# Decoder step: tokens turned once in the loading stage, with the inverse norm spread by a product with ones

## The chip, the cores and the metric

The kernel runs on one core of a Trainium2 chip. The metric is the device time of one execution in microseconds (us), the median of several. For this kernel a difference under 0.2% (about 3.9 us) can't be told from no change.

## The reference, cut to what matters

The program is one layer of a decoder for 256 prompt tokens and 64 sample tokens together (T = 320), width D = 2048. Only its first two steps bear on the change:

```python
def rmsnorm(x, g):
    xf = x.astype(F32)
    y = xf * lax.rsqrt(jnp.mean(xf * xf, axis=-1, keepdims=True) + NORM_EPS)
    return (y * g.astype(F32)).astype(x.dtype)
...
    h = rmsnorm(x, lp['ln_mix_g'])
    proj = h @ lp['w_in']
```

What follows is an RWKV-7 recurrence, latent attention, an output projection, cross-attention to 256 memory tokens, and a mixture of experts (32 experts, each with three weight matrices of 2048 x 512).

## The kernel before

The kernel is written engine by engine: each stage is a block in which the queues of TensorE (PE), VectorE (DVE), ScalarE (ACT), GpSimd (POOL) and SyncE (SP) are listed by hand and wait for each other by counting semaphores. A block ends for all engines together, so the next stage starts when the last engine of this one has finished. There is no planner: the order in the text is the order on the engine.

**The loading stage** is `load_front`. The tokens lie in three tiles (`TILE`: 128, 128 and 64 tokens, with all 2048 features in a row: `x`, in the trace `x_tokens`). The stage makes, with features on the partitions: `xT`, the raw tokens turned (in the trace `rw_vak`), which are parked in DRAM for the residual; `hT` (`mix`), normalised and multiplied by the norm's weights; and `hT` as a high part `S.xh` (`x_high`) in a reduced format and a remainder `S.xl` (`x_low`). Both halves feed the projection, which makes three products for each tile of weights: high by high, high by low, low by high.

- SP issues the identity, the three tiles of tokens, the first two tiles of the projection's weights (L318), and the rest of the tables (L172).
- PE turns each raw tile, 16 transposes into four banks `p_r` (`turn_raw`, L189), the old shift state (28 small transposes, L209) and the vector rows, among them the norm's weights (L213). Then it turns each tile a second time after scaling (`turn_scaled`, L202), into three banks `p_s`.
- ACT issues the small loads, squares and sums each tile and takes the root (`square`, L239 and L241), copies the raw turned tiles out of PSUM (`copies`, L247), and rounds `hT` to its high part (`high`, L253).
- DVE takes the reciprocal of the root (L270), scales the tile's rows by it (`scale`, L273), multiplies the turned scaled tile by the norm's weights while it takes it out of PSUM (`gain`, L279), subtracts for the low part (`low`, L285), and last copies the shift state (L302).

**The projection stage** is `project_in`, the block behind it: 35 tiles of weights (s = 0 to 34), two buffers. For each, ACT rounds the high part (`split`, L457), DVE subtracts the low part (`split`, L528), and PE makes three times 16 products of 320 columns (L426, L428, L431). SP first issues two small weights and the parking of `xT` (L362 to L364), then each next tile of weights as soon as DVE has made the low part of the tile that lies in its buffer:

```python
                sp.dma_start(S.xT_dram, S.xT[:, :, :].rearrange("p t n -> p (t n)")).then_inc(parked, 16)
                for s in range(RAWS, total):
                    sp.wait_ge(low, s - RAWS + 1)
                    load_in_weights(sp, d, S, s)
```

Of the kernel before, what the change touches and what calls it, by code (L numbers as in the profile page):

```python
# [12 lines left out]
ALU = mybir.AluOpType  # L13
# [129 lines left out]
def load_front(nc, d, S):  # L143

    with ExitStack() as ctx:
# [4 lines left out]
        ss = sb("x_ss", [128, 3]); root = sb("x_root", [128, 3]); inv = sb("x_inv", [128, 3])  # L150
        p_r = [ps(f"p_r{i}") for i in range(4)]; p_s = [ps(f"p_s{i}") for i in range(3)]; p_v = ps("p_v")
        cleared = sem("cleared"); rows_in = sem("vec_in"); x_in = [sem(f"x_in{i}") for i in range(3)]; prev_in = sem("prev_in"); tables_in = sem("tables_in"); ident_in = sem("ident_in")
        vec_turned = sem("vec_turned"); vec_done = sem("vec_done"); prev_turned = sem("prev_turned"); prev_done = sem("prev_done")
        raw_turned = sem("raw_turned"); raw_copied = sem("raw_copied"); squared = sem("x_squared"); rooted = sem("x_rooted"); inverted = sem("x_inverted"); scaled = sem("x_scaled")
        turned = sem("x_turned"); gained = sem("x_gained"); high_made = sem("x_high_made"); low_made = sem("x_low_made")
# [6 lines left out]
        with nc.Block() as block:  # L162
# [12 lines left out]
            @block.gpsimd  # L175
            def _(pool):
                pool.memset(rows[:, :, :], 0.0).then_inc(cleared, 1)
                pool.memset(S.eps[:, :], EPS).then_inc(cleared, 1)

            @block.tensor  # L180
            def _(pe):
                def turn_raw(i):
                    n = TILE[i]
                    pe.wait_ge(x_in[i], 16)
                    for q in range(4):
                        if i:
                            pe.wait_ge(raw_copied, 4 * (i - 1) + q + 1)
                        for t in range(4):
                            ins = pe.transpose(p_r[q][:, n * t:n * t + n], x[0:n, i, 512 * q + 128 * t:512 * q + 128 * t + 128], S.ident[0:n, 0:n])  # L189
                        ins.then_inc(raw_turned, 1)  # L190

                def turn_scaled(i):
                    n = TILE[i]
                    pe.wait_ge(scaled, i + 1)
                    for q in range(4):
                        use = 4 * i + q
                        if use >= 3:
                            pe.wait_ge(gained, use - 2)
                        elif use == 2:
                            pe.wait_ge(vec_done, 1)  # L200
                        for t in range(4):
                            ins = pe.transpose(p_s[use % 3][:, n * t:n * t + n], x[0:n, i, 512 * q + 128 * t:512 * q + 128 * t + 128], S.ident[0:n, 0:n])  # L202
                        ins.then_inc(turned, 1)

                pe.wait_ge(ident_in, 16)
                turn_raw(0)
                pe.wait_ge(prev_in, 16)
                for t, (c, n) in enumerate(cols):
                    ins = pe.transpose(p_v[0:n, 8 * t:8 * t + 8], prev[:, c:c + n], S.ident[0:8, 0:8])  # L209
                ins.then_inc(prev_turned, 1)  # L210
                pe.wait_ge(rows_in, 16 * (len(VECTORS) + 2))
                for i in range(2):
                    ins = pe.transpose(p_s[2][:, 128 * i:128 * i + 128], rows[:, i, :], S.ident)  # L213
                ins.then_inc(vec_turned, 1)
                turn_raw(1)
                turn_scaled(0)
                turn_raw(2)
                turn_scaled(1)
                turn_scaled(2)

            @block.scalar
            def _(act):
                act.dma_start(prev[:, :], d['state_rwkv_shift'][0]).then_inc(prev_in, 16)
# [19 lines left out]
                def copies(i):  # L243
                    n = TILE[i]
                    for q in range(4):
                        act.wait_ge(raw_turned, 4 * i + q + 1)
                        act.copy(xT[:, 4 * q:4 * q + 4, at[i]:at[i] + n], p_r[q][:, 0:4 * n].rearrange("p (t n) -> p t n", t=4)).then_inc(raw_copied, 1)  # L247

                def high(i):
                    n = TILE[i]  # L250
                    act.wait_ge(gained, 4 * i + 4)
                    act.wait_ge(squared, 3)
                    act.copy(S.xh[:, :, at[i]:at[i] + n], hT[:, :, at[i]:at[i] + n]).then_inc(high_made, 1)  # L253

                square(0)
                copies(0)
                square(1)
                square(2)
# [3098 lines left out]
```

## Time and profile before

| | |
|---|---|
| median of 3 runs | 1936.49 us (1932.57 to 1936.51) |
| the profiled execution, its own time | 1926.11 us |
| its span (first to last instruction) | 1924.4 us |
| PE busy | 1795.4 us, 93% of the span |
| DVE busy / ACT busy | 687.8 us (36%) / 481.6 us (25%) |
| loading stage | to 33.84 us of the span |
| projection, first product | 35.65 us |

Times inside the trace are counted from the start of the span. In a timeline row the first number is the start, the second the time from it to the end of the last instruction merged into the row; "xN" is how many there are, and brackets hold how long the engine was idle before and what released it. Where several rows of one engine overlap, the next instruction has started while the one before is still finishing. L numbers are lines of the kernel.

### The profile page before, as it was taken

What the parts mean: (1) busy time and instruction counts of PE and PEld (TensorE: products, weight loads), DVE (VectorE), ACT (ScalarE), POOL (GpSimd) and SP (SyncE); (2) the same over time, 40 slices, a digit from 0 to 9 for tenths busy, and PEclk for the clock granted to TensorE, in tenths of its full rate; (3) what the DMA queues carried; (4) which work ended last, traced back from release to release, by engine and by line L of the source; (5) the groups of instructions that cost most, each with busy time, mean ns of one, the idle gap of its engine ahead of it and who ended that gap; (6) DMA issues with size and microseconds to landing.
All of it is one profiled execution on the core that took longest, in us unless ns stands there. A gap on an engine that the chain in (4) does not pass through costs nothing. (4 is left out here: it accounts for less than half of the span.)

```text
span 1924.4 us, 35948 instructions
## 1 busy us (share of the span) xinstructions
PE 1795.4 (93%) x15607; PEld 1232.4 (64%) x15607; DVE 687.8 (36%) x1296; ACT 481.6 (25%) x836; POOL 111.7 (6%) x115
## 2 busy tenths in 40 slices
PE   5999998997989999998999999999999999999995
PEld 5999987875667799786455554554554544555442
DVE  4437776545568443753411111111111111111113
ACT  4446654441223322732311011011110000000001
POOL 0000002300101000000000000000000000000000
PEclk8999999998999999999999999999999999999998
DMA  7644550224535772547899999999999999999997
GB/s 225 162 127 127 136 132 11 69 36 126 167 117 221 235 191 67 184 136 303 309 385 428 421 424 427 424 421 418 422 421 427 421 425 420 419 426 423 422 426 267
DMA packets 191391, 545.99 MB, mean 284 GB/s; under 512 B 39227, under 2 KB 146844, under 8 KB 163566
## 3 DMA queue, kind: packets, MB, share of 16 engines
q1 hardware_dynamic: 184080, 518.03, 70.4%
q0 software_dynamic: 6768, 26.09, 4.4%
q8 instruction: 84, 1.38, 0.3%
q10 hardware_dynamic: 438, 0.32, 0.1%
q14 instruction: 21, 0.17, 0.0%
HBM read 524.86 MB, written 28.06 MB: 287 GB/s over the span
## 5 line engine op out<-in xcount | busy, mean ns | idle before, releaser
L2976 PE MATMUL p_u<-w_expert,xgT 128*64 128x256 f32 x2048 | 239.2, 387 | 26.7 <-DMA w_expert<-in_w_up_dram 26.6
L2976 PE MATMUL p_g<-w_expert,xgT 128*64 128x256 f32 x2048 | 232.1, 379 | 1.7 <-DVE xgT L3079 0.9
L2976 PEld LDWEIGHTS p_u<-w_expert,xgT 128*64 128x64 f32 x2048 | 148.9, 140 | 108.7 <-DMA w_expert<-in_w_up_dram 33.7
L2992 PE MATMUL p_y<-w_expert,hidT 128*64 128x512 f32 x960 | 217.5, 595 | 0.5 <-DVE hidT L3091 0.5
L2976 PEld LDWEIGHTS p_g<-w_expert,xgT 128*64 128x64 f32 x2048 | 146.7, 137 | 89.1 <-issue 18.4
L2944 PE MATMUL p_xg<-low,slot_sel 128*64 128x512 f32 x768 | 177.1, 596 | 0.0
L2992 PEld LDWEIGHTS p_y<-w_expert,hidT 128*64 128x64 f32 x960 | 66.3, 137 | 125.4 <-issue 124.7
L3084 DVE CAST row<-rowf 128x1 int32<-128x1 f32 x32 | 4.9, 154 | 356.9 <-POOLq L3225 356.9
L3171 ACT ACTIVATE act_g<-p_g 128x256 f32<-128x256 f32 x32 | 12.3, 383 | 442.0 <-PE p_u L2976 442.0
L2944 PEld LDWEIGHTS p_xg<-low,slot_sel 128*64 128x64 f32 x768 | 52.3, 137 | 79.4 <-issue 73.6
L426 PE MATMUL in_acc<-x_high,w_in_high 128*128 128x320 f32 (+2 forms) x560 | 93.2, 319 | 8.2 <-ACT w_in_high L457 8.2
L3222 POOL DMA_INDIRECT x_dram<-y_slots,row x31 | 48.3, 1557 | 870.7 <-DVE y_slots L3095 870.7
L528 DVE TENSOR_TENSOR w_in_low<-w_in_raw,w_in_high 128x2048 fp32r<-128x2048 f32 (+2 forms) x35 | 77.8, 2228 | 52.4 <-ACT w_in_high L457 52.3
L3079 DVE COPY xgT<-p_xgT 128x512 f32<-128x512 f32 x32 | 22.1, 692 | 206.4 <-PE p_xgT L2959 206.4
L426 PEld LDWEIGHTS in_acc<-x_high,w_in_high 128*128 128x128 f32 (+2 forms) x560 | 84.9, 187 | 11.4 <-ACT w_in_high L457 8.9
L431 PE MATMUL in_acc<-x_high,w_in_low 128*128 128x320 f32 (+2 forms) x560 | 88.0, 309 | 1.6 <-DVE w_in_low L528 1.6
L428 PE MATMUL in_acc<-x_low,w_in_high 128*128 128x320 f32 (+2 forms) x560 | 87.8, 309 | 0.0
L431 PEld LDWEIGHTS in_acc<-x_high,w_in_low 128*128 128x128 f32 (+2 forms) x560 | 83.2, 185 | 2.3 <-DVE w_in_low L528 2.1
L428 PEld LDWEIGHTS in_acc<-x_low,w_in_high 128*128 128x128 f32 (+2 forms) x560 | 83.3, 185 | 0.2
L457 ACT CAST w_in_high<-w_in_raw 128x2048 fp32r<-128x2048 f32 (+2 forms) x35 | 64.7, 1852 | 10.6 <-DMA w_in_raw<-in_w_in_dram 4.6
L3164 ACT COPY xg<-p_xg 128x512 f32<-128x512 f32 x32 | 18.7, 585 | 190.7 <-PE p_xg L2944 190.7
L3095 DVE COPY y_slots<-p_y 128x512 f32<-128x512 f32 x32 | 22.1, 692 | 97.2 <-PE p_y L2992 97.2
(601 smaller groups left out, 2439.1 us busy)
## 6 DMA issues: line engine op xcount, KB each, us to landing
w_expert<-in_w_gate_dram SPq DMA_DIRECT2D x64, 2048.0 KB, 21.6
w_expert<-in_w_up_dram SPq DMA_DIRECT2D x64, 2048.0 KB, 23.2
w_expert<-in_w_down_dram SPq DMA_DIRECT2D x60, 2048.0 KB, 19.8
w_in_raw<-in_w_in_dram SPq DMA_DIRECT2D x32, 1024.0 KB, 5.8
ho_raw<-in_w_out_dram SPq DMA_DIRECT2D x12, 1024.0 KB, 6.5
q_lat<-in_w_out_dram SPq DMA_DIRECT2D x4, 1024.0 KB, 8.1
mem_k_s<-in_cache_mem_k_dram SPq DMA_DIRECT2D x8, 512.0 KB, 7.5
mem_v_s<-in_cache_mem_v_dram SPq DMA_DIRECT2D x8, 512.0 KB, 11.5
```

The lines of the kernel that those rows point to most:

```text
L426: pe.matmul(o, wh[s % 2][:, k, 0:m], S.xh[:, k, :], start=(k == 0), stop=False)
L428: pe.matmul(o, wh[s % 2][:, k, 0:m], S.xl[:, k, :], start=False, stop=False)
L431: ins = pe.matmul(o, wl[s % 2][:, k, 0:m], S.xh[:, k, :], start=False, stop=(k == DT - 1))
L457: act.copy(wh[s % 2][:, :, 0:m], S.raw[s % RAWS][:, :, 0:m]).then_inc(high, 1)
L528: dve.tensor_tensor(wl[s % 2][:, :, 0:m], S.raw[s % RAWS][:, :, 0:m], wh[s % 2][:, :, 0:m], ALU.subtract).then_inc(low, 1)
L2944: mm = pe.matmul(p_xg[SL * h:SL * h + SL, 512 * b:512 * b + 512], sel[:, i, SL * h:SL * h + SL], S.h3[:, i, 8 * h + 4 * b:8 * h + 4 * b + ...
L2976: mm = pe.matmul(acc[SL * h:SL * h + SL, 0:FF // 2], xgT[:, t, g // 2, :], w[g][:, FF * t + FF // 2 * h:FF * t + FF // 2 * h + FF // 2], s ...
L2992: mm = pe.matmul(p_y[SL * h:SL * h + SL, 512 * b:512 * b + 512], hidT[:, j, g, :], tile, start=(g == 0 and j == 0), stop=(g == 1 and j == 1))
L3079: dve.tensor_copy(xgT[:, 0:4, :, :].rearrange("p t h s -> p (t h s)"), p_xgT[:, 0:512]).then_inc(xgT_v, 1)
L3095: dve.tensor_copy(y[:, 0:512], p_y[:, 0:512]).then_inc(y_v, 1)
L3164: act.copy(xg[:, 4:8, :].rearrange("p t q -> p (t q)"), p_xg[:, 512:1024]).then_inc(xg_a, 1)
L3222: pool.indirect_dma_start(out=halves, out_offset=bass.IndirectOffsetOnAxis(ap=row[:, 0:1], axis=0), in_=y[:, :], in_offset=None, bounds_ch ...
```

## The change

In the loading stage the tokens are turned once. The second turning (`turn_scaled`) and the scaling of the rows (`scale`) are gone. Instead DVE makes a diagonal matrix of the tile's inverse norms from the identity (`inverse`), PE multiplies a matrix of ones by it (`spread_inverse`), so that each of the 128 partitions of a bank `p_inv` holds the inverse norm of every token, and DVE makes `hT` from the turned raw tile `xT`, the norm's weights as a scalar for each partition, and `p_inv`, with one instruction for each of 16 feature tiles (`gain`: 48 instructions, 32 of 128x128 and 16 of 128x64). The norm's weights come by a small load of their own, first on ACT's queue, and are turned first on PE. A root of a constant stands ahead of the squares on ACT. DVE copies the first turned tile out of PSUM in ACT's place; ACT copies the other two and, at the end of its queue, the shift state and the vectors in DVE's place. The raw turned tiles go round five banks. The high part of the first tile of weights (`S.wh0`) is made by ACT at the end of the loading stage and no longer at the start of the projection.

```diff
-        ss = sb("x_ss", [128, 3]); root = sb("x_root", [128, 3]); inv = sb("x_inv", [128, 3])
-        p_r = [ps(f"p_r{i}") for i in range(4)]; p_s = [ps(f"p_s{i}") for i in range(3)]; p_v = ps("p_v")
+        ss = sb("x_ss", [128, 3]); root = sb("x_root", [128, 4]); inv = sb("x_inv", [128, 3])
+        diag, ones = S.al[:, 0:3, 0:128], S.al[:, 3, 0:128]
+        gain_rows, gain_columns = S.al[0:DT, 4, 0:128], S.al[:, 5, 0:DT]
+        RING = 5
+        p_r = [ps(f"p_r{i}") for i in range(RING)]; p_inv = [ps("p_inv0"), ps("p_inv1")]; p_v = ps("p_v")
+        p_prev, p_gain, p_rows = p_v[:, 0:224], p_v[:, 224:224 + DT], p_v[:, 256:512]
...
+                pool.memset(ones, 1.0).then_inc(cleared, 1)
 
             @block.tensor
             def _(pe):
+                def bank_free(u):
+                    if RING <= u < RING + 4:
+                        pe.wait_ge(first_copied, u - RING + 1)
+                    elif u >= RING + 4:
+                        pe.wait_ge(raw_copied, u - RING - 3)
+
                 def turn_raw(i):
                     n = TILE[i]
                     pe.wait_ge(x_in[i], 16)
                     for q in range(4):
-                        if i:
-                            pe.wait_ge(raw_copied, 4 * (i - 1) + q + 1)
+                        u = 4 * i + q
+                        bank_free(u)
                         for t in range(4):
-                            ins = pe.transpose(p_r[q][:, n * t:n * t + n], x[0:n, i, 512 * q + 128 * t:512 * q + 128 * t + 128], S.ident[0:n, 0:n])
+                            ins = pe.transpose(p_r[u % RING][:, n * t:n * t + n], x[0:n, i, 512 * q + 128 * t:512 * q + 128 * t + 128], S.ident[0:n, 0:n])
                         ins.then_inc(raw_turned, 1)
 
-                def turn_scaled(i):
+                def spread_inverse(i):
                     n = TILE[i]
-                    pe.wait_ge(scaled, i + 1)
-                    for q in range(4):
-                        use = 4 * i + q
-                        if use >= 3:
-                            pe.wait_ge(gained, use - 2)
-                        elif use == 2:
-                            pe.wait_ge(vec_done, 1)
-                        for t in range(4):
-                            ins = pe.transpose(p_s[use % 3][:, n * t:n * t + n], x[0:n, i, 512 * q + 128 * t:512 * q + 128 * t + 128], S.ident[0:n, 0:n])
-                        ins.then_inc(turned, 1)
+                    pe.wait_ge(diagonal, i + 1)
+                    if i == 2:
+                        pe.wait_ge(gained, DT)
+                    pe.matmul(p_inv[i % 2][:, 0:n], ones[0:n, :], diag[0:n, i, 0:n], start=True, stop=True).then_inc(spread, 1)
 
                 pe.wait_ge(ident_in, 16)
+                pe.wait_ge(gain_in, 16)
+                pe.transpose(p_gain, gain_rows, S.ident[0:DT, 0:DT]).then_inc(gain_turned, 1)
                 turn_raw(0)
+                pe.wait_ge(cleared, 3)
+                spread_inverse(0)
+                turn_raw(1)
+                pe.wait_ge(gain_kept, 1)
                 pe.wait_ge(prev_in, 16)
                 for t, (c, n) in enumerate(cols):
-                    ins = pe.transpose(p_v[0:n, 8 * t:8 * t + 8], prev[:, c:c + n], S.ident[0:8, 0:8])
+                    ins = pe.transpose(p_prev[0:n, 8 * t:8 * t + 8], prev[:, c:c + n], S.ident[0:8, 0:8])
                 ins.then_inc(prev_turned, 1)
+                spread_inverse(1)
+                turn_raw(2)
...
-                turn_raw(1)
-                turn_scaled(0)
-                turn_raw(2)
-                turn_scaled(1)
-                turn_scaled(2)
+                spread_inverse(2)
 
             @block.scalar
             def _(act):
+                act.dma_start(gain_rows, d['ln_mix_g'][0].rearrange("(r n) -> r n", n=128)).then_inc(gain_in, 16)
                 act.dma_start(prev[:, :], d['state_rwkv_shift'][0]).then_inc(prev_in, 16)
...
                 def copies(i):
                     n = TILE[i]
                     for q in range(4):
-                        act.wait_ge(raw_turned, 4 * i + q + 1)
-                        act.copy(xT[:, 4 * q:4 * q + 4, at[i]:at[i] + n], p_r[q][:, 0:4 * n].rearrange("p (t n) -> p t n", t=4)).then_inc(raw_copied, 1)
+                        u = 4 * i + q
+                        act.wait_ge(raw_turned, u + 1)
+                        act.copy(xT[:, 4 * q:4 * q + 4, at[i]:at[i] + n], p_r[u % RING][:, 0:4 * n].rearrange("p (t n) -> p t n", t=4)).then_inc(raw_copied, 1)
 
                 def high(i):
                     n = TILE[i]
-                    act.wait_ge(gained, 4 * i + 4)
+                    act.wait_ge(gained, DT * i + DT)
                     act.wait_ge(squared, 3)
                     act.copy(S.xh[:, :, at[i]:at[i] + n], hT[:, :, at[i]:at[i] + n]).then_inc(high_made, 1)
 
+                act.activation(root[:, 3:4], S.eps[:, :], ACT.Sqrt)
                 square(0)
-                copies(0)
                 square(1)
+                copies(1)
                 square(2)
-                copies(1)
+                copies(2)
                 high(0)
-                copies(2)
                 high(1)
                 high(2)
+                act.wait_ge(prev_turned, 1)
+                act.wait_ge(vec_turned, 1)
+                src = p_prev.rearrange("p (t b) -> p t b", b=8)
+                for lo, hi, n in ((0, 24, 128), (24, 26, 96), (26, 28, 128)):
+                    act.copy(S.prev[0:n, lo:hi, :], src[0:n, lo:hi]).then_inc(prev_done, 1)
+                act.copy(S.vectors[:, :], p_rows).then_inc(vec_done, 1)
+                act.wait_ge(S.raw_in[0], 16)
+                act.copy(S.wh0[:, :, 0:IN_TILES[0][2]], S.raw[0][:, :, 0:IN_TILES[0][2]]).then_inc(first_high, 1)
 
             @block.vector
             def _(dve):
-                def scale(i):
+                def inverse(i):
                     n = TILE[i]
                     dve.wait_ge(rooted, i + 1)
                     dve.reciprocal(inv[0:n, i:i + 1], root[0:n, i:i + 1]).then_inc(inverted, 1)
                     dve.wait_ge(inverted, i + 1)
-                    dve.wait_ge(raw_turned, 4 * i + 4)
-                    dve.tensor_scalar(x[0:n, i, :], x[0:n, i, :], inv[0:n, i:i + 1], None, ALU.mult).then_inc(scaled, 1)
-
-                def gain(i):
+                    dve.tensor_scalar(diag[0:n, i, 0:n], S.ident[0:n, 0:n], inv[0:n, i:i + 1], None, ALU.mult).then_inc(diagonal, 1)
+
+                def gain(i, tiles):
                     n = TILE[i]
-                    for q in range(4):
-                        dve.wait_ge(turned, 4 * i + q + 1)
-                        dve.tensor_tensor(hT[:, 4 * q:4 * q + 4, at[i]:at[i] + n], p_s[(4 * i + q) % 3][:, 0:4 * n].rearrange("p (t n) -> p t n", t=4),
-                                          S.vec("ln_mix")[:, 4 * q:4 * q + 4].unsqueeze(2).to_broadcast([128, 4, n]), ALU.mult).then_inc(gained, 1)
+                    dve.wait_ge(spread, i + 1)
+                    for t in tiles:
+                        if i:
+                            dve.wait_ge(raw_copied, 4 * (i - 1) + t // 4 + 1)
+                        else:
+                            dve.wait_ge(first_copied, t // 4 + 1)
+                        dve.scalar_tensor_tensor(hT[:, t, at[i]:at[i] + n], xT[:, t, at[i]:at[i] + n], gain_columns[:, t:t + 1], p_inv[i % 2][:, 0:n], ALU.mult, ALU.mult).then_inc(gained, 1)
 
                 def low(i):
                     n = TILE[i]
                     dve.wait_ge(high_made, i + 1)
                     dve.tensor_tensor(S.xl[:, :, at[i]:at[i] + n], hT[:, :, at[i]:at[i] + n], S.xh[:, :, at[i]:at[i] + n], ALU.subtract).then_inc(low_made, 1)
 
-                scale(0)
-                dve.wait_ge(vec_turned, 1)
-                dve.tensor_copy(S.vectors[:, :], p_s[2][:, 0:256]).then_inc(vec_done, 1)
-                dve.wait_ge(vec_done, 1)
-                scale(1)
-                gain(0)
-                scale(2)
-                gain(1)
+                dve.wait_ge(gain_turned, 1)
+                dve.tensor_copy(gain_columns, p_gain).then_inc(gain_kept, 1)
+                dve.wait_ge(gain_kept, 1)
+                for q in range(4):
+                    dve.wait_ge(raw_turned, q + 1)
+                    dve.tensor_copy(xT[:, 4 * q:4 * q + 4, 0:128], p_r[q][:, :].rearrange("p (t n) -> p t n", t=4)).then_inc(first_copied, 1)
+                inverse(0)
+                gain(0, range(8))
+                inverse(1)
+                gain(0, range(8, DT))
+                gain(1, range(12))
+                inverse(2)
+                gain(1, range(12, DT))
+                gain(2, range(DT))
                 low(0)
-                gain(2)
                 low(1)
                 low(2)
-                dve.wait_ge(prev_turned, 1)
-                src = p_v[:, 0:224].rearrange("p (t b) -> p t b", b=8)
-                for lo, hi, n in ((0, 24, 128), (24, 26, 96), (26, 28, 128)):
-                    dve.tensor_copy(S.prev[0:n, lo:hi, :], src[0:n, lo:hi]).then_inc(prev_done, 1)
 
 
 FR = mybir.dt.float32r
...
-        wh = [sb(f"w_in_high{i}", [128, DT, 128], FR) for i in range(2)]; wl = [sb(f"w_in_low{i}", [128, DT, 128], FR) for i in range(2)]
+        wh = [S.wh0, sb("w_in_high1", [128, DT, 128], FR)]; wl = [sb(f"w_in_low{i}", [128, DT, 128], FR) for i in range(2)]
...
-                    pe.wait_ge(high, s + 1)
+                    if s:
+                        pe.wait_ge(high, s)
...
-                split(0)
+                split(1)
                 act.wait_ge(one_mu_made, 1)
                 for s, (t, c, m) in enumerate(IN_TILES):
-                    if s + 1 < total:
+                    if 1 < s + 1 < total:
                         split(s + 1)
...
-                    dve.wait_ge(high, s + 1)
+                    if s:
+                        dve.wait_ge(high, s)
...
+                    S.wh0 = sb3("w_in_high0", [128, DT, 128], FR)
```

## Rows read from the trace of the kernel before

**Rows 1.** The page: shares of the chain that ended last, by engine.

```profile
PE 29%; DMA 19%; DVE 1%; issue 0%; ACT 0%; DVEq 0%
```

**Rows 2.** The timeline of DVE, loading stage and start of the projection.

```profile
12.13 0.16 DVE L270 RECIPROCAL x_inv<-x_root 128x1 f32<-128x1 f32 x1 [12.13 <-ACT x_root L241]
12.33 1.29 DVE L273 TENSOR_SCALAR x_tokens<-x_tokens,x_inv 128x2048 f32<-128x2048 f32 x1
...
20.02 2.48 DVE L279 TENSOR_TENSOR mix<-p_s,vectors 128x512 f32<-128x512 f32 x4
...
29.99 3.42 DVE L285 TENSOR_TENSOR x_low<-mix,x_high 128x2048 fp32r<-128x2048 f32 x2
33.33 0.51 DVE L302 COPY mix_prev<-p_v 128x192 f32<-128x192 f32 x3
35.63 3.43 DVE L528 TENSOR_TENSOR w_in_low<-w_in_raw,w_in_high 128x1536 fp32r<-128x1536 f32 x2 [1.14 <-ACT w_in_high L457]
```

**Rows 3.** The timeline of ACT, the same stretch.

```profile
7.20 1.28 ACT L239 ACT_TABLE_LOAD   x1 [7.20 <-issue]
8.49 1.91 ACT L239 ACTIVATE x_high<-x_tokens 128x2048 fp32r<-128x2048 f32 x1
...
11.81 0.29 ACT L241 ACTIVATE x_root<-x_ss,eps 128x1 f32<-128x1 f32 x1
...
34.12 1.47 ACT L457 CAST w_in_high<-w_in_raw 128x1536 fp32r<-128x1536 f32 x1 [2.97 <-PEq L162]
...
48.85 1.90 ACT L457 CAST w_in_high<-w_in_raw 128x2048 fp32r<-128x2048 f32 x1 [4.06 <-DMA w_in_raw<-in_w_in_dram]
```

**Rows 4.** The timeline of PE, the same stretch.

```profile
7.43 3.64 PE L189 MATMUL p_r<-tables_sb,x_tokens 128*128 128x128 f32 x16 [7.43 <-DMA x_tokens<-in_x_prompt_dram]
11.01 1.91 PE L209 MATMUL p_v<-tables_sb,prev_rows 8*128 8x8 f32 x28
...
18.55 1.47 PE L202 MATMUL p_s<-tables_sb,x_tokens 128*128 128x128 f32 x12
...
35.65 3.84 PE L426 MATMUL in_acc<-x_high,w_in_high 128*96 128x320 f32 x16 [6.03 <-ACT w_in_high L457]
...
51.06 2.51 PE L426 MATMUL in_acc<-x_high,w_in_high 128*128 128x320 f32 x16
```

**Rows 5.** DMA issues by line: size, and time from issue to landing.

```profile
x_tokens<-in_x_prompt_dram SPq DMA_DIRECT2D x1, 1024.0 KB, 9.7
```

**Rows 6.** SP's timeline at the start of the projection.

```profile
34.99 0.42 SPq L364 DMA_DIRECT2D xT_dram<-rw_vak  x1
37.41 0.39 SPq L318 DMA_DIRECT2D w_in_raw<-in_w_in_dram  x1
```

**Rows 7.** DMA issues, those of rows 6 with their landing.

```profile
xT_dram<-rw_vak SPq DMA_DIRECT2D x1, 2560.0 KB, 10.3
w_in_raw<-in_w_in_dram SPq DMA_DIRECT2D x1, 1024.0 KB, 11.4
```

**Rows 8.** Timeline of DVE elsewhere: small instructions behind each other.

```profile
960.94 0.86 DVE L3063 TENSOR_SCALAR slot_sel<-slot_of,shift,pos_of 128x128 f32<-128x128 f32 x3
418.93 0.88 DVE L1372 SCALAR_TENSOR_TENSOR rw_arena<-rw_arena,vectors,low 128x256 f32<-128x256 f32 x2
45.22 0.27 DVE L588 SCALAR_TENSOR_TENSOR lora<-in_acc,vectors,lora 96x56 f32<-96x56 f32 x1
45.41 0.23 DVE L589 SCALAR_TENSOR_TENSOR lora<-mix_prev,vectors,lora 96x8 f32<-96x8 f32 x1
```

**Rows 9.** Groups of DVE by line and shape: busy us, mean ns of one.

```profile
L3063 DVE TENSOR_SCALAR slot_sel<-slot_of,shift,pos_of 128x128 f32 x93 | 26.7, 344 | 0.7 <-issue 0.7
```

**Rows 10.** Stretches of PE: busy time, granted clock, DMA share, GB/s.

```profile
28.50:35.60 7.10, 0.68 (x4) 0.50 0.08 11
35.60:38.70 3.10, 3.05 (x12) 0.54 1.06 348
38.70:52.00 13.30, 13.30 (x93) 1.00 1.04 328
```

More of the change, by code:

```diff
@@ L149, in load_front @@
         rows = sb("vector_rows", [128, 2, 128]); x = sb("x_tokens", [128, 3, D]); prev = sb("prev_rows", [8, RPROJ])
-        ss = sb("x_ss", [128, 3]); root = sb("x_root", [128, 3]); inv = sb("x_inv", [128, 3])
-        p_r = [ps(f"p_r{i}") for i in range(4)]; p_s = [ps(f"p_s{i}") for i in range(3)]; p_v = ps("p_v")
+        ss = sb("x_ss", [128, 3]); root = sb("x_root", [128, 4]); inv = sb("x_inv", [128, 3])
[4 more added lines that the diff above has]
+        p_prev, p_gain, p_rows = p_v[:, 0:224], p_v[:, 224:224 + DT], p_v[:, 256:512]
+        gain_in = sem("gain_in"); gain_turned = sem("gain_turned"); gain_kept = sem("gain_kept"); diagonal = sem("x_diagonal"); spread = sem("x_spread"); first_high = sem("first_w_high"); first_copied = sem("first_copied")
         cleared = sem("cleared"); rows_in = sem("vec_in"); x_in = [sem(f"x_in{i}") for i in range(3)]; prev_in = sem("prev_in"); tables_in = sem("tables_in"); ident_in = sem("ident_in")
         vec_turned = sem("vec_turned"); vec_done = sem("vec_done"); prev_turned = sem("prev_turned"); prev_done = sem("prev_done")
-        raw_turned = sem("raw_turned"); raw_copied = sem("raw_copied"); squared = sem("x_squared"); rooted = sem("x_rooted"); inverted = sem("x_inverted"); scaled = sem("x_scaled")
-        turned = sem("x_turned"); gained = sem("x_gained"); high_made = sem("x_high_made"); low_made = sem("x_low_made")
+        raw_turned = sem("raw_turned"); raw_copied = sem("raw_copied"); squared = sem("x_squared"); rooted = sem("x_rooted"); inverted = sem("x_inverted"); gained = sem("x_gained"); high_made = sem("x_high_made"); low_made = sem("x_low_made")
         names = dict(w0='rwkv_w0', a0='rwkv_a0', k_k='rwkv_k_k', k_a='rwkv_k_a', gn_g='rwkv_gn_g', gn_b='rwkv_gn_b', ln_mix='ln_mix_g', q_norm='mla_q_norm_g',
@@ L210, in _ @@
                 ins.then_inc(prev_turned, 1)
+                spread_inverse(1)
+                turn_raw(2)
                 pe.wait_ge(rows_in, 16 * (len(VECTORS) + 2))
                 for i in range(2):
-                    ins = pe.transpose(p_s[2][:, 128 * i:128 * i + 128], rows[:, i, :], S.ident)
+                    ins = pe.transpose(p_rows[:, 128 * i:128 * i + 128], rows[:, i, :], S.ident)
                 ins.then_inc(vec_turned, 1)
-                turn_raw(1)
-                turn_scaled(0)
```

## The prediction

> **What bounds the kernel now.** I read the page first. PE is busy 93% of the span, and the chain that ended last runs through PE for 29% and through DMA for 19% of it, none of it in the loading stage [rows 1]: that chain starts only where the experts begin. This says nothing against the loading stage. The stages are blocks, each begins when the one before has ended, and every later transfer is released by an instruction of its own stage, so what the head of the program gains is handed down whole unless something fixed in time catches it.
>
> So I read the timelines of the three engines over the first 52 us. DVE is the engine that ends the loading stage: from the first reciprocal at 12.13 it works nearly without a break up to the low parts and the copies of the shift state, the last of which ends at 33.33 + 0.51 = 33.84 [rows 2]. ACT starts the first cast of the projection 0.28 later, at 34.12, and PE its first product at 35.65, when this cast of 1.47 is done [rows 3, 4]. So the first product hangs on two things: DVE's last instruction, and then ACT's cast.
>
> A third limit stands 15 us further on. The third tile of weights (s = 2) is issued at 37.41 and lands 11.4 later, at 48.81 [rows 6, 7]. ACT casts it from 48.85 to 50.75 [rows 3], and PE begins its products at 51.06 [rows 4]. PE works without a gap up to there, so weights and PE are ready within 0.3 us of each other. Ahead of this transfer in SP's queue stands the parking of `xT`, 2560 KB, issued at 34.99 and landed 10.3 later, at 45.3 [rows 6, 7]. From there to 48.81 are 3.5 us for 1024 KB, some 300 GB/s: the weights go when the parking has gone, not when they are issued. And the parking is issued when the block begins.
>
> **The change, part by part.**
>
> *Up to the first diagonal.* Tile 0 is turned as before: 16 transposes in 3.64, the last at 11.07 [rows 4], one bank each 0.91. DVE now copies each bank. Its nearest row is the multiply out of PSUM, four of 128x512 in 2.48, so about 0.6 each [rows 2]; that is less than 0.91, only the last copy shows, and it ends near 11.7. The root: ACT's table load at 7.20 takes 1.28, then the new root of a constant 0.29, then square and accumulator 11.81 - 8.49 less the second table load of the same length, 2.0, then the root 0.29 [rows 3], with one more issue at the head of its queue (0.4, as SP's [rows 6]): 11.5. It is not late. Then the reciprocal and its hand-over 0.2 (12.13 to 12.33 [rows 2]), the diagonal 0.3 (a 128x128 scalar instruction: 0.26 to 0.34 [rows 8, 9]), and one product of 128 columns with its hand-overs. The trace of before has no such product alone; a transpose takes 0.12 to 0.23 [rows 4], a product of 320 columns 0.16 to 0.24; twice to three times that with two hand-overs, 0.3 to 0.9, I take 0.6. DVE begins its first `gain` at 12.8 (12.5 to 13.3).
>
> *The 48 multiplies.* A single instruction lasts 0.344 at 128x128 [rows 9], but the next one starts before it is done: three take 0.86, so a start every (0.86 - 0.34) / 2 = 0.26 [rows 8]. The same form as the new one stands at 256 elements: two in 0.88 with 0.48 for the last, 0.40 apart, and at 56 elements: 0.19 apart [rows 8]. On that line 128 elements come to 0.26 and 64 to 0.20. 32 x 0.26 + 16 x 0.20 = 11.6. Bounds: from below, the multiply out of PSUM at 0.60 for 512 elements [rows 2] leaves 0.07 over one element per nanosecond or so, which gives 0.20 and 0.13, together 8.5; from above, no overlap at all, 0.344 and 0.28, together 15.5.
>
> *What else DVE does.* Two more inverses of 0.45 each: 0.9. The low parts as before: 128x2048 and 128x1024 in 3.42 [rows 2], the first 128x2048 by the same rate 2.2: 5.6. The high parts on ACT (under 2 us each) come while DVE still multiplies, and are hidden by it. The copies of the shift state (0.51) and of the vectors leave DVE.
>
> *PE behind it.* The second product with ones stands behind the turning of tile 1 and the 28 small transposes. From 12.8: 16 transposes at 0.12 or 0.23, 2.0 to 3.6 (the higher figure is that of tile 0, the lower that of the later turnings [rows 4]), then 1.91 [rows 4], then the product: ready at 17.2 to 18.9. DVE wants it at 12.8 + 16 x 0.26 + 0.45 = 17.4. A wait of 0 to 1.5; I take 0.3. Nothing but this product is late if PE is slow here. The second turnings that vanish (48 transposes) had DVE waiting at either end, and are worth nothing of their own.
>
> *The end of the stage.* 12.8 + 11.6 + 0.9 + 5.6 + 0.3 = 31.2, against 33.84: 2.6 earlier. ACT's queue must end before that: its last high part can start at 25.6, then about 1.0, the three small copies and the vectors about 1.0, and the cast of the first weights 1.47 [rows 3]: 29.1. These are hidden by DVE's low parts with 2 us to spare; without that cover they would cost up to 3.5. The first weights wait for no transfer: x of tile 1, issued right behind tile 0 and ahead of them, takes 9.7 to land [rows 5], and they follow long before 27.
>
> *The start of the projection.* The block begins 2.6 earlier, and PE finds the first high part made: 1.53 (34.12 to 35.65) more, 4.1 in all, for the first product. [...]
>
> *But PE then runs into the third tile.* Its load comes only 2.6 earlier, with the parking. So PE waits 1.3 or so before s = 2, and its products there start (50.75 - 2.6) + 0.1 = 48.25, or 2.8 earlier than 51.06. The head start of the cast made early is given back, but for 0.2. From there on, the same order of the same work runs 2.8 earlier to the end.
>
> Sum: 2.6 + 0.2 = 2.8. The profiled execution took 1926.1, so 1923.3 for it; the median of the runs shown is 10.4 above that execution, and 1936.5 - 2.8 = 1933.7. This is under 0.2% (3.9), about what a measurement of this kernel can tell from no change.
>
> [...] In rows 8 and 9, small DVE instructions start 0.26 apart though each lasts 0.344. [...]
>
> **Rivals.**
>
> 1. *Small instructions don't overlap* when each of them waits for and raises a semaphore and reads PSUM. 48 at full length cost 15.5 and not 11.6: the stage ends at 35.1, 1.3 later than before, and the third tile comes as much later less 0.2: 1937.6. It turns a gain into a loss where the mean of the 48 passes 0.30 us, and would cost over 0.2% (2.8 + 3.9 over 48) only from 0.38, more than a 128x128 instruction lasts in rows 9. For it: no row here has such an instruction with both PSUM and a wait. Against: rows 8 overlap, and the multiply out of PSUM with a semaphore each (0.60 for 512) does too. Chance 0.13, 0.07 of it beyond 0.2%.
> 2. *The weights don't wait for the parking.* If the third tile lands by its own issue (which comes 3.7 earlier, as the low part no longer waits for a cast), PE keeps its 4.1: 1932.4, faster by 0.21%. For it: the transfers share 16 engines. Against: landing times in a row, and 300 GB/s for what is left. Chance 0.12.
> 3. *The multiplies are cheaper than I say*, near 8.5. Then PE's second product sets DVE's pace, and of the 3.1 about 1.8 are left: 4.6 earlier, 1931.9. Chance 0.12.
> 4. [...] Chance 0.13.
>
> The forecast, 1933.7, has 0.48; its own range is 1932.5 to 1935.2, from the bounds of the first product and of the second wait.
>
> **How the numbers follow.** Rivals 2 and 3 lie just past 0.2%: 0.24 for faster, and 0.02 more for both at once, 0.26. Slower by over 0.2%: the far end of rival 1, 0.07. The same: 0.48, 0.13 and the 0.06 of rival 1 that stays inside, 0.67. The range for 8 in 10 reaches to rivals 2 and 3 together, 1930.3, and to rival 1 at full length, 1938.0.
>
> **What the changed profile would show.** DVE's first `gain` near 12.8, starts 0.26 apart; DVE's last instruction near 31.2 and ACT's cast of the first weights done by 29 or 30; PE's first product of the projection near 31.6; the third tile landing near 46.2, with PE idle about 1.3 before its products. The prediction is wrong if the 48 multiplies take over 14 or under 10, if the stage ends on ACT, or if the third tile lands without regard to the parking.

## The result, and the profile after

The changed kernel is slower: a median of 1945.3 us in 12 runs (1938.5 to 1953.0) against 1936.5 for the kernel before in its 12 (1932.6 to 1942.6), a ratio of 1.0038 [1.0025, 1.0051]. I had forecast 1933.7, and gave "slower by over 0.2%" a chance of 0.07. The head of the program does nearly what was worked out; the time is lost 260 us behind it, in code that the change doesn't touch.

First the head. The timeline of the changed kernel up to the first weights, ACT, DVE, PE and SP together (start us, duration, engine, line, operation, count, idle before it):

```profile
12.26 0.29 DVE L291 TENSOR_SCALAR rw_al<-tables_sb,x_inv 128x128 f32<-128x128 f32 x1
12.70 0.46 PE L208 MATMUL p_inv<-rw_al 128*128 128x128 f32 x2 [1.27 <-DVE rw_al L291]
...
13.19 2.15 DVE L301 SCALAR_TENSOR_TENSOR mix<-rw_vak,rw_al,p_inv 128x128 f32<-128x128 f32 x8 [0.64 <-PE p_inv L208]
...
15.66 5.25 DVE L301 SCALAR_TENSOR_TENSOR mix<-rw_vak,rw_al,p_inv 128x128 f32<-128x128 f32 x20
...
21.18 4.18 DVE L301 SCALAR_TENSOR_TENSOR mix<-rw_vak,rw_al,p_inv 128x128 f32<-128x128 f32 x20
...
25.28 5.61 DVE L306 TENSOR_TENSOR x_low<-mix,x_high 128x2048 fp32r<-128x2048 f32 x3
...
26.95 1.49 ACT L282 CAST w_in_high<-w_in_raw 128x1536 fp32r<-128x1536 f32 x1
...
31.22 4.38 PE L449 MATMUL in_acc<-x_high,w_in_high 128*96 128x320 f32 x16 [9.22 <-PEq L166]
```

The 48 multiplies take 2.15 + 5.25 + 4.18 = 11.6 us. DVE is done at 25.28 + 5.61 = 30.89, against 33.84 [rows 2], ACT at 28.44 and so hidden, and PE's first product of the projection comes at 31.22 instead of 35.65 [rows 4].

Then the third tile of weights. DMA issues with their KB and median time to landing, at the start of the projection:

```profile
xT_dram<-rw_vak SPq DMA_DIRECT2D x1, 2560.0 KB, 11.5
w_in_raw<-in_w_in_dram SPq DMA_DIRECT2D x2, 1024.0 KB, 14.8
```

and the timeline over 44 to 55 us:

```profile
44.81 2.51 PE L454 MATMUL in_acc<-x_high,w_in_low 128*96 128x320 f32 x16
...
47.17 1.90 ACT L480 CAST w_in_high<-w_in_raw 128x2048 fp32r<-128x2048 f32 x1 [6.21 <-DMA w_in_raw<-in_w_in_dram]
...
49.12 2.61 PE L449 MATMUL in_acc<-x_high,w_in_high 128*128 128x320 f32 x16 [1.80 <-ACT w_in_high L480]
```

PE waits 1.80 for the cast, which waited for the transfer, as forecast (1.3). The parking of `xT` takes 11.5 us and not 10.3 [rows 7], and the tile's products start at 49.12: 1.94 earlier than before [rows 4], not 2.8. From the parking's issue to the cast of this tile are 15.1 us, where before had 13.9 (e1, below: 14.1); e2 and e5, with the same head as the changed kernel, have 15.0 and 15.3, e5 with a parking of 10.5. So it is the two transfers together that take some 1 us longer; why is not shown.

Now the start of the same PE product in each kernel, less its start in the profile of before shown above, at places named by their time there (us, worked out from the traces; e1 is a second profile of the kernel before, e2 one of the changed kernel):

```
place in before       e1      after      e2
   51.06            +0.75    -1.94    -0.88
  311.42            +0.73    -1.93    -0.89   first products of the heads stage
  317.03            +1.03    +1.05    +1.55
  342.03            +0.99    +1.47    +3.77
  357.34            +1.01    +4.19    +6.22
  381.00            +1.56    +9.41   +12.16
  543.48            +0.70   +12.77   +12.24
  616.46            +8.66   +21.17   +20.62
 1500.07            +7.68   +20.55   +21.77
```

The gain of the head is whole up to 311.42. It is gone 6 us later, and by 381 some 11 are lost. The step between 543 and 616 (sample attention) is none of the change's: e1 has it too. The profile of before that I predicted from was the one profile of all in which each step of that stage took 11.3 to 12.0 us and not 13.1; the others have three short stops of PE in each step, where neighbouring matmuls start 0.4 to 0.5 apart. These are 5 or 6 matmuls from each other, and at the same matmuls of the work, give or take one, in e1 and in the changed kernel: so they aren't block ends. Against e1 the changed kernel loses most of its time in one place: 10.5 by 381 (in e2 12.2). This profile of it loses another 4.2 between 381 and 543, most of it while the clock was granted at 0.50 over 547.3 to 554.1 of its own time; e2 loses 0.9 there.

That place, in the timeline of PE (matmuls alone). After:

```profile
309.49 0.99 PE L873 MATMUL hb<-rw_vak,rw_al 64*32 64x64 f32 x57 [0.76 <-PEq L381]
...
310.38 0.82 PE L880 MATMUL hb<-rw_vak,rw_al 64*32 64x64 f32 x59
313.50 1.47 PE L880 MATMUL hb<-rw_vak,rw_al 64*32 64x64 f32 x128 [2.29 <-issue]
316.96 1.19 PE L880 MATMUL hb<-rw_vak,rw_al 64*32 64x64 f32 x65 [1.99 <-issue]
318.08 1.98 PE L842 MATMUL hb<-mix,rw_vak 64*64 64x64 f32 x63
320.97 0.37 PE L842 MATMUL hb<-mix,rw_vak 64*64 64x64 f32 x1 [0.91 <-issue]
```

Before, the same products:

```profile
311.42 0.99 PE L849 MATMUL hb<-rw_vak,rw_al 64*32 64x64 f32 x57 [0.76 <-PEq L359]
...
312.31 1.70 PE L856 MATMUL hb<-rw_vak,rw_al 64*32 64x64 f32 x146
315.80 1.30 PE L856 MATMUL hb<-rw_vak,rw_al 64*32 64x64 f32 x106 [1.79 <-issue]
317.03 0.57 PE L818 MATMUL hb<-mix,rw_vak 64*64 64x64 f32 x22
319.25 0.91 PE L818 MATMUL hb<-mix,rw_vak 64*64 64x64 f32 x42 [1.65 <-issue]
```

PE stops in mid-run, put down to "issue": it waits for nothing that the profile shows. The stops stand 128 matmuls apart (128; 65 + 63; before 106 + 22). Each matmul has its weight load (the page counts 15566 of both), so that is 256 instructions. The DMA view of 308 to 320 us in the changed kernel (40 slices of 0.3 us; share of the engines, GB/s):

```profile
DMA  0000000000100000000000100000000000200000
GB/s 0 0 0 0 0 0 0 0 0 0 55 0 0 0 0 0 0 0 0 0 0 0 55 0 0 0 0 0 0 0 0 0 0 0 55 0 0 0 0 0
...
q8 instruction: 3, 0.05, 1.6%
```

Nothing moves but three packets on the instruction queue, 0.05 MB in all, so about 16 KB each, at 311.1, 314.6 and 318.2, some 3.5 us apart. I call the 256 instructions from one stop to the next a block. PE runs through a block of these short matmuls (32 to 64 columns) in about 1.5 us (128 in 1.47), where 16 products of 320 columns take 2.51. So it uses up its stream faster than the packets come here, and stands for 2.29 and 1.99 us at the first two ends of a block. That a packet holds one block is my reading of the two spacings.

Where a block ends depends, by this reading, on how many instructions PE has had since its start; the experiments below test it. The pages of both kernels count them (PE's x):

```profile
PE 1804.7 (93%) x15566; PEld 1238.9 (64%) x15566; DVE 690.8 (35%) x1333; ACT 479.6 (25%) x836; POOL 112.3 (6%) x116
```

Before, it was 15607 of each kind. The second turnings took 48 away; the three products with ones (two matmuls each in the trace) and the turned gain brought 7: 41 pairs fewer, 82 instructions, all in the loading stage. Every block boundary behind it stands 41 matmuls later in the work. In the heads stage, counted from its product at 309.49, a boundary now falls after 127 matmuls and stops PE; before, the boundaries fell after 86, which shows no stop, and 214, which does.

### The profile page after: what moved, and what is told of

Read it like the earlier page. It is cut to its first block and busy times, and to the rows that moved or that the text cites. A ratio compares the mean times of both kernels' runs of the same rounds, so it can differ in the third digit from the quotient of the medians.

```text
span 1946.8 us, 35908 instructions
## 1 busy us (share of the span) xinstructions
PE 1804.7 (93%) x15566; PEld 1238.9 (64%) x15566; DVE 690.8 (35%) x1333; ACT 479.6 (25%) x836; POOL 112.3 (6%) x116
## 6 DMA issues: line engine op xcount, KB each, us to landing
mem_v_s<-in_cache_mem_v_dram SPq DMA_DIRECT2D x8, 512.0 KB, 10.9
```

## The experiments

Two theories had to be told apart. The **count theory**: the time is lost because PE's block boundaries moved. The **phase theory**: it is lost because the work comes at another time (the granted clock, or some transfer); the recorded texts call it the clock theory and speak of moments at which the clock can change. The traces show such moments: in the changed kernel the granted clock steps between 1.00 and 0.50 at 315.15, 325.39, 342.45, 349.28, 352.69 and 356.10, in the kernel before at 14.55, 17.97, 28.21 and 38.45, so 3.4 us apart or 2, 3 or 5 times that. I speak of *before's places* where the stops in the heads stage come after the same products as before, and of *after's places* likewise. In the table that stretch runs from the products at 311.42 to the same later product (382.85 before); the stops are the spacings of over 0.6 us between neighbouring matmuls at block boundaries there, which may include a wait for DVE. Each median is over 6 to 12 runs; each ratio is against runs of before timed beside the kernel, whose medians went from 1936.5 to 1939.2, so ratios compare better than medians.

```
kernel                     median  ratio [95%]               stretch us  clock  stops, sum us
before                     1936.5                               71.43    0.98   3, 5.2
e1  before again           1938.2  1.0003 [0.9991, 1.0015]      72.26    0.98   3, 6.2
e8  before, SP late        1936.8  0.9994 [0.9981, 1.0008]      73.56    0.95   3, 5.6
e10 before + 128 turns     1947.3  1.0046 [1.0028, 1.0065]      76.56    0.91   3, 5.9
e3  after + 82 on PE       1940.1  1.0015 [1.0003, 1.0027]      74.95    0.93   3, 5.5
e5  after + 41 turns       1931.3  0.9968 [0.9955, 0.9981]      75.26    0.89   3, 6.0
e7  e5, parking late       1932.5  0.9978 [0.9965, 0.9990]      72.88    0.95   3, 5.1
e11 after + 20 turns       1939.7  1.0007 [0.9995, 1.0019]      76.30    0.89   3, 5.5
after                      1945.3  1.0038 [1.0025, 1.0051]      82.77    0.86   6, 10.9
e2  after again            1943.1  1.0033 [1.0018, 1.0047]      84.47    0.86   6, 10.5
e13 after, all of it late  1946.4  1.0046 [1.0029, 1.0064]      82.60    0.86   6, 10.5
e4  before + 174 on PE     1962.2  1.0133 [1.0112, 1.0155]      77.29    0.91   6, 9.6
e6  before + 87 turns      1951.4  1.0076 [1.0055, 1.0096]      78.82    0.87   6, 9.5
e9  before + 46 and 64     1950.1  1.0055 [1.0039, 1.0071]      84.15    0.84   6, 10.3
```

**Both kernels again** (no edit).

> The kernel before, unchanged, for a second profile and as a measure of how far two timings of one program lie apart. Every theory: ratio 1.000 within 0.002. What its profile tells: whether the sample attention steps take 11.3 to 12 us each, as in the first profile of before (instruction stream theory: yes, they do in every execution of this program), and whether the stretches of low clock lie at the same places (if the low clock falls by chance from run to run, they will not).

> The changed kernel, unchanged. The change as such: +0.45% over the kernel before. Instruction stream theory (PE's later work stands elsewhere in its instruction stream, and starves at the same places in every execution): the sample attention steps take 13.1 us each again, each with three stalls of 0.4 us on PE. Chance theory (stalls and low clock fall where they fall): steps of 11.3 to 13.1 mixed, and the ratio nearer 1.002.

The ratio holds, 1.0033. The steps of sample attention take 13.1 us in both profiles, and e1 is the kernel before. So the count theory in its first form, which looked for the loss in that stage (it stands so in the texts of the first four runs), is wrong there: the loss lies in the heads stage, and the rest of the runs are read in that stage. The view of stretches, PE alone (us, busy and count, granted clock, DMA share, GB/s), e1 and then e2:

```profile
312.15:384.41 72.26, 63.08 (x2073) 0.98 0.20 47
```

and e2:

```profile
310.54:395.01 84.47, 72.12 (x2074) 0.86 0.18 41
```

The same products take 9 us more of PE's busy time, at a lower mean clock, and 3 us more of idle time.

**The count put back at PE's head.** The changed kernel with as many instructions on PE as before:

```diff
+                for _ in range(82):
+                    pe.nop().then_inc(filler, 1)
                 pe.wait_ge(ident_in, 16)
```

> The changed kernel with 82 instructions that do nothing at the head of PE's queue, where PE is idle for 7 us: as many as its loading stage has fewer, so that all of PE's later instructions stand where they stood before. Instruction stream theory: the stalls in the sample attention go, the steps take 11.3 to 12 us, and the time is that of before less the 2 us won at the head: 0.998 to 1.001. Clock theory (the work is shifted by 2 us against the moments at which the clock can change): as the changed kernel, 1.004.

The stops are back at before's places. But PE's first instruction came at 13.53, so that each filler cost about 0.16 us, and the first product of the projection came at 38.29, 7.1 later than in the changed kernel. Even so it runs in 1940.1: 3.1 us less than e2, timed beside it, and 5.2 less than the first timing of the changed kernel. The ratio, 1.0015, is above the 0.998 to 1.001 that I had expected.

**The count moved the other way.** The kernel before with 174 fillers at the same place. 256 instructions are a block, and 256 - 82 = 174, so its boundaries stand where the changed kernel's do.

> The kernel before with 174 such instructions at the head of PE's queue: 174 and not 82 fewer is the same place within a block of 256 instructions (16 KB, the size of one load of instructions in the trace). The loading stage is as before. Instruction stream theory with blocks of 256: the stalls of the changed kernel appear in the sample attention, steps of 13.1 us, and the time rises by 8 us or more, 1.004. [...]

Six stops, at after's places. The fill took 27 us (PE's first matmul came at 27.59), where PE is idle for 7.4 [rows 4], and made the head 16 to 17 late; the total says little, the stretch does: 77.29 against 72.26, with 3.4 more of stops.

**The count put back where PE is idle.** 41 small transposes into a used bank, late in the loading stage:

```diff
                 spread_inverse(2)
+                pe.wait_ge(raw_copied, 8)
+                for _ in range(41):
+                    pe.transpose(p_r[0][:, 0:8], x[0:8, 0, 0:128], S.ident[0:8, 0:8])
```

> The changed kernel with 41 small transposes into a bank that nobody reads, behind PE's last product of the loading stage, where PE is idle for 9 us: the 82 instructions by which its loading stage is shorter, this time without a cost at the head. Instruction stream theory: the third tile's products start at 49.1 as in the changed kernel, the stops at the start of the heads are two and not three, and the time is 2 us under the kernel before or level with it: 0.998 to 1.001. Rival (only the low clock, which falls by chance, makes the changed kernel slow): 1.003 to 1.004 as the changed kernel.

This is the clean test: the head does the changed kernel's work and nothing is seen to wait for the turns. They end at 27.40, and the first product of the projection comes at 32.16, between that of the changed kernel (31.22) and that of e2 (32.45). Its PE timeline, loading stage and projection:

```profile
22.87 4.53 PE L231 MATMUL p_r<-tables_sb,x_tokens 8*128 8x8 f32 x41
32.16 4.54 PE L452 MATMUL in_acc<-x_high,w_in_high 128*96 128x320 f32 x16 [4.75 <-PEq L166]
```

and at the heads stage:

```profile
311.49 1.70 PE L883 MATMUL hb<-rw_vak,rw_al 64*32 64x64 f32 x146
315.02 1.30 PE L883 MATMUL hb<-rw_vak,rw_al 64*32 64x64 f32 x106 [1.83 <-issue]
316.25 0.79 PE L845 MATMUL hb<-mix,rw_vak 64*64 64x64 f32 x22
```

146, 106 and 22, as before. The median is 1931.3, ratio 0.9968 [0.9955, 0.9981]: 14 us below the changed kernel, from PE work that computes nothing, and faster than both kernels.

**The same done to the kernel before,** to put it at after's places: 87 turns behind `turn_scaled(2)`, with `pe.wait_ge(raw_copied, 12)` ahead of them.

> The kernel before with 87 small transposes in the same way, at the end of PE's loading queue, in its idle 6 us: 174 instructions, so PE's later instructions stand in their blocks of 256 as in the changed kernel. Nothing else is changed. Instruction stream theory: three stops at the start of the heads, at the matmuls at which the changed kernel stops, three more in the next 70 us, and 5 to 10 us in all: 1.003 to 1.005. Rival: the kernel before, 1.000.

Its PE timeline at the heads stage:

```profile
319.03 0.82 PE L859 MATMUL hb<-rw_vak,rw_al 64*32 64x64 f32 x59
321.88 1.68 PE L859 MATMUL hb<-rw_vak,rw_al 64*32 64x64 f32 x128 [2.02 <-issue]
325.61 1.19 PE L859 MATMUL hb<-rw_vak,rw_al 64*32 64x64 f32 x65 [2.06 <-issue]
```

59, 128, 65: the changed kernel's stops, in the kernel before. The turns made the head 5.1 later than e1 (41.36 against 36.28), and the stretch is 6.6 longer. The ratio of 1.0076 is above the 1.003 to 1.005 expected, since those left out the late head.

**The parking moved back, and a delay on SP.** Both ran beside e5 and e6. In e7, a copy of e5, the parking is issued behind the third and fourth tile of weights:

```diff
-                sp.dma_start(S.xT_dram, S.xT[:, :, :].rearrange("p t n -> p (t n)")).then_inc(parked, 16)
...
+                    if s == RAWS + 2:
+                        sp.dma_start(S.xT_dram, S.xT[:, :, :].rearrange("p t n -> p (t n)")).then_inc(parked, 16)
```

> The kernel of 41 small transposes, and the parking of xT issued behind the third and fourth tile of weights in SP's queue, not ahead of them. If the third tile waits for the parking, it now lands near 39, PE goes from the second tile to the third with no gap near 47.3 and not 49.1, and the time falls by 1.8 us more: 0.001 under the kernel of 41 transposes. If it waits for its own issue, nothing changes.

PE at the third tile, timeline of e7:

```profile
45.80 2.51 PE L458 MATMUL in_acc<-x_low,w_in_high 128*96 128x320 f32 x16
48.15 2.51 PE L453 MATMUL in_acc<-x_high,w_in_high 128*128 128x320 f32 x16
```

and of e5:

```profile
50.22 2.61 PE L452 MATMUL in_acc<-x_high,w_in_high 128*128 128x320 f32 x16 [1.79 <-ACT w_in_high L483]
```

The wait of 1.79 is gone and the products come 2.1 earlier, as my reading of rows 6 and 7 has it: with the parking ahead of them the weights come late. In the total the two can't be told apart (1932.5 and 1931.3). e8 delays the kernel before by 12 fillers at the head of SP's queue:

```diff
+                for _ in range(12):
+                    sp.nop().then_inc(filler, 1)
```

> The kernel before with twelve instructions that do nothing at the head of SP's queue (0.157 us each in the run with 82 on PE, so 1.9 us): all of it starts 1.9 us later, and PE's instruction stream is as before. Clock theory (where the work stands against the moments at which the clock can change decides on 5 us or more): the stretches of low clock at 340 to 450 us are others than the kernel before has, and the time moves by more than the 1.9 us. Instruction stream theory: 1.001, the 1.9 us and no more, and the two stops of the kernel before.

PE's first matmul came 0.9 to 1.0 later, but the heads stage only 0.5 later than in e1, and 1.2 than in the shown profile of before; so e8 hardly tests the phase theory.

**Three more counts.** e9 has 46 fillers at PE's head and 64 turns at the end (46 + 128 = 174); e10 has 128 turns, 256 instructions, a whole block, as a control that delays and doesn't move the boundaries; e11 is the changed kernel with 20 turns.

> The kernel before with 46 instructions that do nothing at the head of PE's queue (7.2 us at 0.157 each, inside its idle 7.4) and 64 small transposes at the end of its loading queue (128 instructions): 174 in all, as in the run with 87 transposes, but with a cost at the head of under 2 us. Instruction stream theory: PE's first products of the projection within 2 us of 35.65, three stops at the start of the heads and three in the next 70 us, and 5 to 8 us in all: 1.003 to 1.005. Rival (the filler itself, which is PE work, made the run with 87 slow): as the head, 1.000 to 1.001.

> The kernel before with 128 small transposes at the end of PE's loading queue: 256 instructions, one whole block, so everything behind stands in the blocks as in the kernel before. The filler takes longer than PE's idle 6 us, so the head is 7 to 9 us late. Instruction stream theory: two stops at the start of the heads, and nothing lost but the head: 1.004. Rival (fillers slow later stages as such): the head and 6 us more, 1.007 or over, though it has more filler than the run with 87.

> The changed kernel with 20 small transposes, 40 instructions: the block boundaries fall 20 matmuls later in the stream than in the changed kernel. Instruction stream theory: at the start of the heads stops 20 matmuls on, two of 2 us, and the third falls together with the wait that PE has there anyway; the time between the changed kernel and the one with 41 transposes, 0.998 to 1.002. If only the exact place of before helps, 1.003 to 1.004.

e9 made the head 3 to 5 us late, more than expected, and has after's stops. e10 has before's stops, with the first product of the projection 9.4 later than e1's: no stop is added by the delay, and its median of 1947.3 is 8.2 above the runs of before timed beside it, no more than that delay. Its stretch is 4.3 longer than e1's, at a clock of 0.91, with the same stops. e11 came out at 1939.7, ratio 1.0007 [0.9995, 1.0019], between the changed kernel and e5. It has three stops in the stretch, at neither kernel's places. Its stops came 20 matmuls earlier in the work than after's and not later, as I had expected; I had the sign wrong, since extra instructions ahead bring each boundary forward. So its boundary falls 107 matmuls into the stage, and PE doesn't stop there; it stops at the next two. With 86 (no stop), 107 (none) and 127 (2.29 us) the third stop appears between 107 and 127.

**The changed kernel, late as a whole.** Six chained memsets on GpSimd that SP waits for, ahead of the first loads, and no change on PE:

```diff
+                for i in range(6):
+                    if i:
+                        pool.wait_ge(late, i)
+                    pool.memset(rows[:, :, :], 0.0).then_inc(late, 1)
```

> The changed kernel, all of it about 1.9 to 2.5 us later (six memsets on GpSimd one behind the other, for which SP waits), with PE's instruction stream unchanged. Instruction stream theory: the same six stops, and 1.004 to 1.005, the changed kernel and the delay. Clock theory (the time by which the changed kernel is ahead puts its stops where they drop the clock): the low clock in the first 90 us of the heads falls from 23.9 us to 14 or less, and the time falls by 2 us or more in spite of the delay, to 1.002.

The first product of the projection comes at 34.25, 3.0 later than in the changed kernel. Six stops at the same places, the same clock and stretch. The view of the stretch, e13:

```profile
312.35:394.95 82.60, 71.75 (x2074) 0.86 0.17 42
```

and the changed kernel:

```profile
309.49:392.26 82.77, 71.08 (x2073) 0.86 0.18 41
```

Moving the time leaves the loss as it is; moving the count by 82 takes it away. The three profiles with this stream on PE begin the heads stage at 309.49, 310.54 (e2) and 312.35, and all lose. For these delays the phase theory falls.

## Why the prediction was wrong, point by point

*The multiplies and rival 1: right.* 11.6 us, 0.26 apart at 128 columns, as on rows 8. Rival 1 falls: each of the 48 waits for and raises a semaphore, reads PSUM and lasts 0.34 us (median), and still they start 0.26 apart. Rival 3 falls too: 11.6 is far from 8.5.

*The end of the stage and the first product: right.* 30.89 against 31.2, and 31.22 against 31.6. The second product with ones was ready at 17.1, so the wait of 0.3 didn't come.

*The third tile: mechanism right, size off.* PE's wait was 1.80 where I had 1.3. I had carried the time from the parking's issue to this tile over unchanged, 13.9, and it was 15.1. That leaves 1.9 of the 2.8 against the profile shown, 2.7 against e1 (in e2 0.9 and 1.6). Rival 2 falls: e7 shows that the wait goes when the parking is moved.

*The ends of the range* don't quite follow from the rivals: 2 and 3 together are 1936.5 - 4.1 - 1.8 = 1930.6, not 1930.3, and rival 1 came to 1937.6, not 1938.0. The measured 1945.3 lies outside either way.

*The step that failed:* "From there on, the same order of the same work runs 2.8 earlier to the end", and under it the claim of the first part that "what the head of the program gains is handed down whole unless something fixed in time catches it". Something does lie in wait, fixed not in time but in PE's count of instructions. I costed the 48 transposes that vanish by their time alone, and found them "worth nothing of their own". They are 41 pairs, net, of a stream that is loaded in blocks of 256; taking them away shifts every boundary behind them. Against e1 the sum is: head -2.7 (at 51.06), heads stage 82.77 - 72.26 = +10.5, together +7.8; with e2 for the changed kernel it is -1.6 and +12.2, together +10.6. The medians differ by 8.8. (The two profiled executions differ by 13.5, with the 4.2 behind the heads stage named above, so that the sum fits the medians so closely is in part luck.) No rival had this cause. The 0.13 of rival 4, which stands in the sum for "the same", has no run behind it: what the runs showed in its place is a loss of 8.8.

*How the 10.5 splits.* The stops are 10.9 - 6.2 = 4.7 longer, but e1 has waits for DVE that the changed kernel doesn't have, so PE's idle time grows by 2.5 only (82.77 - 71.08 against 72.26 - 63.08). The other 8.0 are PE's busy time, 71.08 against 63.08 for the same products, at a granted clock of 0.86 over the stretch and not 0.98. The clock parts from e1's within the first 25 us of the stretch. The changed kernel and then e1 (us, PE busy and count, granted clock, DMA share, GB/s):

```profile
309.49:334.49 25.00, 18.53 (x692) 0.80 0.02 4
312.15:337.15 25.00, 18.34 (x818) 1.00 0.02 4
```

In these 25 us all six profiles with six stops have 0.73 to 0.86, and six of the seven with before's places have 1.00. The seventh is e5, with 0.86, as has e11. So it is likely that the extra stops bring the lower clock. But they are not its only cause, e4's stretch (77.29) is hardly longer than e10's (76.56), and no run held the stops and changed the clock alone. That part is argued, not shown.

*What stays open.* Why the granted clock in kernels with the same three stops ranges from 0.89 to 0.98. Why e11, with three stops and a stretch close to e5's (76.30 and 75.26), has a ratio 0.0039 above e5's. Why e5's median is 6.4 below its own comparison runs of the kernel before, when the head gives about 1.6 (at 51.06: -0.84 against e1's +0.75) and its profile shows a stretch 3.0 longer than e1's. And what decides, in one execution or another, whether sample attention's steps take 12 or 13.1 us; of both kernels alike, and in the shown profile of before worth 8 us.

## What to carry to other kernels

Look for "issue" waits inside long runs of tiny matmuls, at constant spacing, with nothing on DMA but the instruction queue: the heads stage here depended on how many instructions PE had had since the start, and an edit far ahead cost more there (10.5 us) than it brought where it was made (2.7). When an edit changes PE's count ahead of such a stage, compare the stops of both traces, and try a few idle-time instructions as padding: 41 small transposes under other work took the changed kernel from 1.0038 to 0.9968, and 20 took it to 1.0007. And profile the kernel before twice before working to 3 us: a single profile can be 8 us off in one stage.

## What the runs showed of the hardware

PE's stream came in packets of about 16 KB, 3.5 and 3.6 us apart while PE stood waiting in the heads stage of the changed kernel; 128 matmuls of 32 to 64 columns with their weight loads, one block, ran in 1.5. A boundary reached 127 matmuls into such a run cost 2.0 to 2.5 us, one at 107 or 86 nothing; the ones behind it 0.7 to 2.7 (spacing of the matmuls on either side of it). A filler on PE that does nothing but raise a semaphore cost about 0.16 us (82 of them put PE's first matmul at 13.53), more than a small transpose of 8 columns at 4.53 / 41 = 0.11.
